# Up projections of two feed-forward layers in pairs of blocks by Strassen's seven products, with the inner tiles kept in memory and the layers split into an up phase and a down phase

## The reference, cut to what matters

```python
m = rms_norm(h, mlp_norm[i])
h = h + jnp.square(jax.nn.relu(m @ w_mlp_up[i])) @ w_mlp_down[i]
```

## Time and profile before

| | |
|---|---|
| time, median of 3 runs | 2839.71 us (2838.74 to 2841.25) |
| the profiled execution | 2841.24 us |
| its span, first to last instruction | 2839.6 us |
| PE busy | 2654.4 us, 93% of the span, 11982 matmuls |
| DVE busy | 1238.9 us, 44% |
| ACT busy | 795.4 us, 28% |
| DMA | 163.25 MB, mean 57 GB/s |
| granted TensorE clock, mean | 0.965 of 2.4 GHz |

### The profile page before, as it was taken

How to read it: one execution, slowest core, us unless ns; L and a number is a source line. 1 busy time by engine, 2 the same in 40 slices (tenths; PEclk the granted TensorE clock), 3 DMA queues, 4 the chain that set the end, 5 groups by cost and what they waited for, 6 DMA issues and landing times.

```text
span 2839.6 us, 31323 instructions
## 1 busy us (share of the span) xinstructions
PE 2654.4 (93%) x11982; PEld 2122.8 (75%) x11982; DVE 1238.9 (44%) x1443; ACT 795.4 (28%) x1115; POOL 61.8 (2%) x87
## 2 busy tenths in 40 slices
PE   7997598999999999999999878999999999999997
PEld 6776555568888888888878656888777788888885
DVE  5227627654423324234464554222576233242346
ACT  4212146652211101112243264111454011111123
POOL 1000000000000000000001200000000000000000
PEclk9998679999999999999999989999999999999998
DMA  5110000012111111111123100111333111111133
GB/s 198 37 37 19 1 0 1 1 60 81 45 52 45 52 52 44 52 44 52 52 82 138 50 0 23 52 45 51 134 104 119 52 45 52 44 52 51 45 126 111
DMA packets 45236, 163.25 MB, mean 57 GB/s; under 512 B 5088, under 2 KB 5120, under 8 KB 45136
## 3 DMA queue, kind: packets, MB, share of 16 engines
q1 hardware_dynamic: 35136, 125.84, 13.2%
q0 software_dynamic: 10032, 36.49, 3.6%
HBM read 144.89 MB, written 16.78 MB: 57 GB/s over the span
## 4 chain that ended last, share of the span: by engine, by line
PE 83%; DVE 8%; ACT 5%; issue 4%; DMA 0%; ACTq 0%; DVEq 0%; POOL 0%; POOLq 0%
PE ps L1681 68%; PE ps L2056 7%; PE ps L1833 1%; PE ps L1904 1%; ACT P L757 1%; PE ps L2010 1%; PE ps L1816 1%; PE ps L1830 1%; PE ps L1934 1%; PE ps L1914 1%; DVE w_lo L941 0%; PE ps L1840 0%; DVE Pb L1275 0%; DVE small L1460 0%; DVE S L1457 0%
## 5 line engine op out<-in xcount | busy, mean ns | idle before, releaser
L1681 PE MATMUL ps<-opP_hi,w_hi 128*128 128x512 f32 x1696 | 526.5, 392 | 5.4 <-DVE w_lo L941 3.8
L1681 PE MATMUL ps<-opP_lo,w_hi 128*128 128x512 f32 x1696 | 524.1, 390 | 0.0
L1681 PE MATMUL ps<-opP_hi,w_lo 128*128 128x512 f32 x1696 | 523.9, 390 | 0.0
L406 ACT ACTIVATE w_hi<-w_stage 128x1024 fp32r<-128x1024 f32 x228 | 239.2, 1049 | 600.3 <-PE ps L1681 598.2
L1681 PEld LDWEIGHTS ps<-opP_hi,w_hi 128*128 128x128 f32 x1696 | 319.4, 189 | 75.6 <-issue 9.8
L1681 PEld LDWEIGHTS ps<-opP_lo,w_hi 128*128 128x128 f32 x1696 | 319.8, 189 | 66.9
L1681 PEld LDWEIGHTS ps<-opP_hi,w_lo 128*128 128x128 f32 x1696 | 319.4, 188 | 66.8
L1681 PE MATMUL ps<-opQ_hi,w_hi 128*128 128x512 f32 x1152 | 357.1, 391 | 7.4 <-DVE w_lo L941 4.3
L1681 PE MATMUL ps<-opQ_hi,w_lo 128*128 128x512 f32 x1152 | 356.1, 390 | 0.0
L1681 PE MATMUL ps<-opQ_lo,w_hi 128*128 128x512 f32 x1152 | 355.8, 390 | 0.0
L941 DVE TENSOR_TENSOR w_lo<-w_stage,w_hi 128x1024 fp32r<-128x1024 f32 x228 | 278.3, 1221 | 100.5 <-ACT w_hi L406 100.2
(11 more groups left out here) (331 smaller groups left out, 2636.7 us busy)
## 6 DMA issues: line engine op xcount, KB each, us to landing
w_stage<-in_w_stream SPq DMA_DIRECT2D x228, 512.0 KB, 3.5
Xre<-x_spill POOLq DMA_DIRECT2D x16, 512.0 KB, 7.3
X<-in_xT POOLq DMA_DIRECT2D x8, 512.0 KB, 10.3
pp_spill<-ppout POOLq DMA_DIRECT2D x1, 4096.0 KB, 13.5
X<-in_xT SPq DMA_DIRECT2D x8, 512.0 KB, 4.4
T<-pp_spill POOLq DMA_DIRECT2D x8, 512.0 KB, 3.5
x_spill<-X POOLq DMA_DIRECT2D x1, 4096.0 KB, 15.1
x_spill<-X POOLq DMA_DIRECT2D x2, 2048.0 KB, 8.5
```

Source lines behind the costliest of these rows:

```text
L406: act.activation(w_hi[:, slot, :], w_stage[:, slot, :], ACT.Copy).then_inc(w_hi_done, 1)
L1681: mm = pe.matmul(ps[:, psum + half, :], weight, operand[:, k, half * HALF:(half + 1) * HALF], start=(begin and x == 0 and weight is wh and ...
```

## The change

Of each layer's up blocks, only the first 4 (layer 1) or the first 8, in halves (layer 2) stay as they are. The other 28 and 24 are taken in pairs. Two output tiles by two halves of the input features make a 2x2 block of the weights, and the two halves of the features by the two halves of the tokens make a 2x2 block of the activations; Strassen's scheme (the form with few additions) makes the 2x2 result from 7 products instead of 8. One product is 4 k-tiles by 3 forms, 12 matmuls of 128x512 in one bank.

- DVE forms 3 sums of the activations plus one in place for each layer (`form_sums`), once; and 4 sums of the weights for each pair (`weight_sum`). ACT and DVE split them into high and remainder (`weight_high`, `weight_low`, each 128x512, 7 for each pair, in place of two full blocks' `w_hi` and `w_lo`).
- DVE adds the products (`combine`, 7 of 128x512 for each pair, one operand in PSUM), ACT first copies one of them (`part_1`). DVE rectifies and scales in one instruction (`rectify`, 128x1024), ACT squares (`pair_square`).
- The squared tile goes from `T` to memory (`h_spill`), started by POOL (`spill`), 512 KB each, 32 tiles a layer. All up blocks and pairs of a layer come first, then all 32 down blocks in 4 chunks of 8; the 8 tiles of a chunk are read back by POOL's queue (`tiles_back`), those of chunk c+1 during chunk c, those of chunk 0 during the last pair, and are split by ACT (`tile_high`) and DVE (`tile_low`).
- The weights of a pair are kept in `X`, so the residual of layer 1 is written to `x_spill` during the w_out blocks, tile by tile, and read back during the last pair and after.
- In UPA ACT's rectify and copy and DVE's remainder go, and DVE's scaling becomes scale and rectify in one; in UPB likewise, and DVE and ACT get the sums and the first weights' parts to make, between the blocks.
- Operands P and Q change their places in the later stages, with the same instructions.

```diff
-B_PP, B_WIN, B_WOUT, B_MLP1 = 0, 2, 18, 26
-B_GATE, B_WIN2, B_MRG, B_WO2 = 90, 98, 108, 132
...
+FF_PLAIN, FF_PAIRS = (4, 8), (14, 12)
...
+            def spill(f, slot, cols=slice(0, S)):
+
+                counts[slot] += 1
+                if counts[slot] > 1:
+                    pool.wait_ge(spilled[slot], 16 * (counts[slot] - 1))
+                pool.dma_start(h_spill[f * P:(f + 1) * P, cols], T[:, slot, cols]).then_inc(spilled[slot], 16)
...
+                    if c == 0:
+                        if order == 0:
+                            pool.wait_ge(ff["lo"], pair_low_no(x, FF_PAIRS[x] - 1, 6))
+                        elif k in (0, 2, 4):
+                            pool.wait_ge(ff["mm"], product_no(x, FF_PAIRS[x] - 1, (1, 2, 4)[k // 2]))
...
+                    if c:
+                        pool.wait_ge(operand_ready, first + 8 * c + order - 1)
...
+            def pair_square(x, p, slot):
+                act.wait_ge(ff["relu"], 2 * pairs_before(x, p) + slot + 1)
+                act.activation(T[:, slot, :], T[:, slot, :], ACT.Square).then_inc(ff["square"], 1)
...
+            def pairs_act(x):
+                for p in range(FF_PAIRS[x]):
+                    weight_high(x, p, 6)
+                    if p:
+                        pair_square(x, p - 1, 1)
+                        act.wait_ge(ff["out"], out_no(x, p - 1, 3))
+                    act.wait_ge(ff["mm"], product_no(x, p, 0))
+                    act.activation(part_1[:, :], ps[:, pair_bank(x, p, 0), :], ACT.Copy).then_inc(ff["first"], 1)
+                    if p + 1 < FF_PAIRS[x]:
+                        for j in range(6):
+                            weight_high(x, p + 1, j)
+                    else:
+                        for order in range(DT):
+                            tile_high(x, HOME[order])
+                    pair_square(x, p, 0)
...
-                act.wait_ge(h0["lin"], n + 1)
-                act.activation(tt, tt, ACT.Relu).then_inc(h0["pos"], 1)
-                act.wait_ge(h0["pos"], n + 1)
-                act.activation(tt, tt, ACT.Square).then_inc(h0["relu"], 1)
-                ffa_high(0, n, n % 2)
...
+                if n == 2:
+                    for k in range(4):
+                        scaled_input(1, k)
+                if 2 <= n < 6:
+                    form_high(1, n - 2)
...
+                v.tensor_tensor(t1_raw[:, k, :], b, a, ALU.subtract).then_inc(ff["sum"], 1)
+                v.scalar_tensor_tensor(t3_raw[:, k, :], d, g, b, ALU.mult, ALU.subtract).then_inc(ff["sum"], 1)
+                v.wait_ge(ff["sum"], sum_no(x, k, 0))
+                v.scalar_tensor_tensor(t2_raw[:, k, :], d, g, t1_raw[:, k, :], ALU.mult, ALU.subtract).then_inc(ff["sum"], 1)
+                v.wait_ge(ff["sum"], sum_no(x, k, 2))
...
+            def slot_free(x, p, slot):
+                v.wait_ge(spilled[slot], 16 * (spills_before(x) + (FF_PLAIN[0] // 2, FF_PLAIN[1])[x] + p))
...
+            def pairs_dve(x):
+                for p in range(FF_PAIRS[x]):
+                    more = p + 1 < FF_PAIRS[x]
+                    if p:
+                        pair_end(x, p - 1)
+                    weight_low(x, p, 6)
+                    if more:
+                        weight_sum(x, p + 1, 0)
+                        weight_sum(x, p + 1, 1)
+                        weight_low(x, p + 1, 0)
+                    else:
+                        tile_low(x, 0, 0, HOME[0])
+                        tile_low(x, 0, 1, HOME[1])
+                    v.wait_ge(ff["first"], pairs_before(x, p) + 1)
+                    combine(x, p, sum_16[:, :], part_1[:, :], part(x, p, 1), 0, 1)
+                    if more:
+                        weight_low(x, p + 1, 1)
+                    combine(x, p, sum_165[:, :], sum_16[:, :], part(x, p, 2), 1, 2)
+                    if more:
+                        weight_low(x, p + 1, 2)
+                        weight_sum(x, p + 1, 2)
+                        weight_sum(x, p + 1, 3)
+                    else:
+                        tile_low(x, 0, 2, HOME[2])
+                    slot_free(x, p, 0)
...
+                    slot_free(x, p, 1)
+                    combine(x, p, T[:, 1, HALF:S], sum_16[:, :], part(x, p, 2), 4)
+                    if more:
+                        weight_low(x, p + 1, 4)
+                    combine(x, p, T[:, 0, HALF:S], sum_165[:, :], part(x, p, 5), 2, 5)
...
+                    rectify(x, p, 0)
+                    if more:
+                        weight_low(x, p + 1, 5)
+                    else:
+                        tile_low(x, 0, 4, HOME[4])
+                        tile_low(x, 0, 5, HOME[5])
...
+                if 2 <= n < 6:
+                    form_sums(1, n - 2)
+                    form_lows(1, n - 2)
+                if n == 6:
+                    first_pair(1, range(3))
+                if n == 7:
+                    first_pair(1, range(3, 6))
...
+            def pairs_pe(x):
+
+                for p in range(FF_PAIRS[x]):
+                    for j, (hi, lo, k0, c0) in enumerate(pair_forms):
+                        if p == 0 and j == 4:
+                            pe.wait_ge(evac_done, (B_DN1, B_DN2)[x])
+                            pe.wait_ge(ff["lo"], third_low_no(x, 3))
+                        if j == 0 and p >= 2:
+                            pe.wait_ge(ff["out"], out_no(x, p - 2, 7))
+                        elif j == 1 and p:
+                            pe.wait_ge(ff["first"], pairs_before(x, p))
+                        elif j and p:
+                            pe.wait_ge(ff["out"], out_no(x, p - 1, (1, 5, 3, 4, 6)[j - 2]))
+                        pe.wait_ge(ff["lo"], pair_low_no(x, p, j))
+                        for k in range(4):
+                            for weight, operand in ((form_hi[j], hi), (form_hi[j], lo), (form_lo[j], hi)):
+                                mm = pe.matmul(ps[:, pair_bank(x, p, j), :], weight[:, wcols(k)], operand[:, k0 + k, c0:c0 + HALF],
+                                               start=(k == 0 and weight is form_hi[j] and operand is hi),
+                                               stop=(k == 3 and weight is form_lo[j]))
+                        mm.then_inc(ff["mm"], 1)
+
...
+                    for n in range(DT):
+                        if n < 2:
+                            pe.wait_ge(ff["out"], out_no(x, FF_PAIRS[x] - 1, (5, 5)[n]))
+                        step(first + n, None, n, n % 2)
```

More of the change, by code:

```diff
@@ new lines, in _ @@
+            for f in range(FF_PLAIN[0]):
+                pool.wait_ge(ff["square"], f + 1)
+                spill(f, f % 2)
+            for p in range(FF_PAIRS[0] - 1):
+                pair_out(0, p, 0)
+                pair_out(0, p, 1)
+            for slot in range(2):
+                pool.wait_ge(spilled[slot], 16 * 4)
+            tiles_back(0, 0)
+            pool.wait_ge(s["spill"], 16 * DT)
+            pool.wait_ge(operand_hi, O_H1 + 6)
+            for k in range(4):
+                pool.dma_start(X[:, k, :], t["x_spill"][k * P:(k + 1) * P, :]).then_inc(tile_landed[k], 16)
@@ new lines, in down_act @@
+            def down_act(x, c):
+                first = (B_DN1, B_DN2)[x] + 8 * c
+                with act.Fori(0, 4) as i:
+                    for j in range(2):
+                        next_high(i * 2 + (first + j), i + first // 2, j)
+                        if c < 3:
+                            act.wait_ge(back[j], i * 16 + 16 * tile_turn(x, c + 1, 0))
+                            settle()
+                            act.activation(tile(h_hi[(c + 1) % 2], i * 2 + j), tile(h_raw[(c + 1) % 2], i * 2 + j), ACT.Copy)\
+                               .then_inc(operand_hi, 1)
@@ L697, in _, with down1 @@
+            third_form_high(0)
+            last_form_high(0)
+            pairs_act(0)
+            for c in range(3):
+                down_act(0, c)
+            def down1(b, turn, n, slot):
+                next_high(b, turn, slot)
+                act.wait_ge(evac_done, b + 1)
+                square_free(2, n)
+                high(opP_hi, tile(X, n), C_PLE, n)
+                square(tile(X, n), 2, n, True)
+            stream(act, B_DN1 + 24, 8, down1)
             next_high(B_GATE, B_GATE // 2, 0)
@@ new lines, in tile_low, with part, combine @@
+            def tile_low(x, c, order, k):
+                v.wait_ge(operand_hi, (O_H1, O_H2)[x] + 8 * c + order + 1)
+                v.tensor_tensor(h_lo[c % 2][:, k, :], h_raw[c % 2][:, k, :], h_hi[c % 2][:, k, :].bitcast(F32), ALU.subtract)\
+                 .then_inc(operand_ready, 1)
+            def part(x, p, j):
+                return ps[:, pair_bank(x, p, j), :]
+            def combine(x, p, out, a, b, after, product=None):
+                if product is not None:
+                    v.wait_ge(ff["mm"], product_no(x, p, product))
+                if after:
+                    v.wait_ge(ff["out"], out_no(x, p, after))
+                v.tensor_tensor(out, a, b, ALU.add).then_inc(ff["out"], 1)
```

(12 more changed lines are left out.)

685 lines of the change are left out of this document (434 added, 251 removed).

## The result

The changed kernel takes 2766.03 us (median of 4 runs, 2764.46 to 2767.58) where the kernel before takes 2839.73 beside it: ratio 0.9737, 95% interval 0.9725 to 0.975, so 73.7 us less. Its profiled execution took 2764.46 us, with a span of 2762.4.

A forecast was written before the change was run, and what follows sets the result against it. PE was taken as the bound in the feed-forward parts; -70.8 - 0.3 - 6.4 + 3.8 + 4 - 0.5 = -70.2 us took the profiled 2841.2 to 2771.0, or about 2770 as median, range 2758 to 2799.

The forecast's parts named there:

- 312 matmuls: Up blocks of both layers: 2496 matmuls become 2184, and those saved go at 0.2268 us each, -70.8 us.
- Layer 1's part: Start of layer 1's feed-forward part: one rectify step fewer ahead of the third up block's `w_lo`, -0.3 us.
- Pairs bound by PE: Pairs of both layers: PE needs 19.05 us a pair, DVE 14.9, ACT 7.1; hand-overs have slack and cost 0.
- UPA, -6.4: UPA to UPB's first block: six blocks take 32.7 us instead of 37.9 and the stage starts 1.2 earlier.
- the ring: UPA's period, scale through ACT and DVE steps back to scale: 6.25 us falls to 5.03, under PE's 5.44.
- UPB, +3.8: UPB: rounds of 7.7 us make PE wait before blocks 4 to 7; last ends at 2209.4 against 2205.6.
- Pair to down, +2 each: Last pair to first down block, twice: DVE reaches tile 4's remainder at 26.4 us, PE needs it at 24.8.
- Last stretch, -0.5: Last down chunk: its tile 7 no longer has a rectify in front, -0.5 us.
- Hand-overs cost: Rival: last pairs' DVE queue held up by landings, UPB and layer 1's start at upper bounds, +20 us; chance 0.18.
- A loss in every product: Rival: PE waits 0.15 to 0.3 us at each of 182 products, 27 to 55 us in all; chance 0.09.
- No change: Rival: a mixture in which losses just meet the gain, with no single mechanism; chance 0.02.
- The rival on the other side: Slower than before: spill landings hold up the pairs, gain gone at 12.5 us, 2907 us at 15; chance 0.05.

The follow-up runs named there:

- e1_eighth_product: Changed kernel with product 7 of each pair computed twice into the same bank, so 312 matmuls are back: 2831.16 us, ratio to before 0.9963.
- e2_upa_two_more: Changed kernel with two more ACT rectify instructions ahead of the square in each of the eight UPA blocks: 2771.69 us, ratio 0.976.
- e8_before_upa_once: Kernel before, with DVE scaling and rectifying in one instruction in UPA and ACT's rectify gone: 2833.81 us, ratio 0.9979.
- e9_before_dn0_by_tile: Kernel before, with layer 2's first down block waiting for its inner tiles one by one, not for all at its start: 2834.08 us, ratio 0.9981.
- e7_dve_8_more: Changed kernel with eight more DVE instructions (128x512, two inputs) in each pair but the last: 2802.7 us, ratio 0.9867.

## Why the prediction was right, and where its terms were off

2770 us was forecast, from 2758 to 2799, and 2766.0 came. On the profiled executions the sum said -70.2 and the traces say -76.8, of which 0.4 us are unchanged code. Term by term:

- *312 matmuls, -70.8.* Right. 0.2267 us in the pairs as in the blocks, and putting the twelve matmuls a pair back costs them again, less the waits that a longer pair hides (e1_eighth_product). Layer 1's part, -36.3, meets the sum's -38.1 - 0.3 + 2 to the tenth, and that is partly luck: the gap at the first down block costs 1.4 and not 2, and one that I had called hidden costs 0.5. There, at the third down block, `w_lo` stands in DVE's queue behind the remainder of the first tile of the next chunk, which DVE waits for 7.4 us. The Trainium skill gives 215.7 ns a matmul (TensorE: Matmul & The Clock Gate, "Wait — 56ns, not 53.3ns?"), by which the term would be an estimated 67.3; no stretch shown here runs at that distance.
- *Pairs bound by PE.* Right. DVE was put at 14.9 us of 19.05, 78%; it has 76 to 78%. The margin is now known: four more instructions are free, eight are not, and about 4.9 us of DVE time is what a pair has left.
- *UPA, -6.4; measured -7.9.* Mechanism right: the ring was the bound (e2_upa_two_more gives it back, e8_before_upa_once gives it alone). The block behind the standstill starts 1.35 us sooner (forecast 1.2), the six behind it take 5.1 us less (forecast 5.2). The failed step is "it takes 8.64 us, since the clock is down after the standstill, and still will": it takes 7.2 us, 1.5 less. Why is open. The standstill before it became shorter, 3.0 us against 4.43, but that is not the cause by itself: in e2_upa_two_more it is 4.37 and the block still takes 7.1.
- *UPB, +3.8; measured +2.8.* Mechanism right, gaps in front of blocks 4 to 7 as forecast, and none behind. The round is 7.39 us (2143.19 to 2150.58) and not 7.7, so a gap costs 1.95 us and not 2.2 (in brackets 1.6), since parts of the round are a tenth or two shorter than I took them. The upper bound, a falling clock in gaps of 2.2 us, did not come: 1.00 throughout.
- *Pair to down, +2 each; measured +1.4 each (1.1 in brackets).* The place was right, tile 4 of the first down block. The mis-sized step is the time at which DVE reaches that tile's remainder: 24.6 us after the last pair's start (at 1023.02 us in the trace) and not 26.4. The first tile is there when it was forecast, 9 us after the start. From then on DVE works through its queue with hardly a wait, 0.35 us in 14.4, so the work in front of tile 4 sets the time; the prediction's own prices for it, 6 remainders, 7 combines and 2 rectifies, make 14.6. What made it 26.4 the prediction doesn't show. The distance of queued landings, 1.8 us a tile from the earlier trace rows, was too large as well. ACT's copies of two of the tiles in the changed kernel, each just after its landing:

```profile
1009.15 1.06 ACT L902 ACTIVATE hA<-hA_raw 128x1024 fp32r<-128x1024 f32 x1 [0.51 <-DMA hA_raw<-h_spill]
1010.48 1.06 ACT L902 ACTIVATE hA<-hA_raw 128x1024 fp32r<-128x1024 f32 x1 [0.27 <-DMA hA_raw<-h_spill]
```

 They come 1.3 us apart, the next ones 1.3 to 1.6. Other traffic doesn't explain the difference: the stretch of the earlier trace rows has 320 GB/s and this one 318.
- *Last stretch, -0.5 beside the matmuls; measured 3 us more than -31.2.* This is the largest miss. About 1.9 of it is the low clock behind the 3.1 us wait, which e9_before_dn0_by_tile measures by taking the wait away; 0.6 is the smaller gap above, and 0.3 that the removed wait of 0.5 us cost 0.8. I had counted the wait at its length in UPB's term and nothing for what it leaves behind.

So nearly all the misses point the same way: the two largest are the clock behind a standstill, 1.5 us for a slow block taken as fixed and 1.9 for one counted at nothing, and the others are rounds and queues taken a little too slow. One slip of the prediction bears on nothing else: its bounds add up to 2759 to 2792 and not to 2795.

*The rivals.* Hand-overs cost 2 x 1.4, 0.5 and 2.8 us, about 6 and not 20. A loss in every product is refuted: no idle time of PE in 1128 matmuls, and none with four more DVE instructions. No change is out. The rival on the other side, the spill holding `slot_free` from a landing of 12.5 us on, did not come: in the pairs a spill lands in 3.5 and 2.9 us (medians of the two layers), at most in 8.7. The Trainium skill (SBUF — State Buffer, "SBUF: two separate sides") warns of transfers started by GpSimd beside a DVE in a two-port mode. DVE is busy for 76% here, with instructions that read two tensors, and none of the spills on POOL's queue comes near 12.5 us. The Trainium skill's fit for one such transfer (DMA: Bandwidth & Descriptors, "Anatomy of one DMA — SWDGE (gpsimd) path") gives an estimated 3.2 us for 512 KB. The spill's median over the whole execution, 3.1, agrees, and the reads' 3.7 is a little above. A longer landing was not tried, so the threshold of 12.5 us is argued and not shown. What e7_dve_8_more does show is the form such a loss would take: pairs whose helper is 0.83 us too slow cost 37 us in all.

*Left open.* What decides between 8.6 and 7.1 us for the slow block, and the -2.2 and +1.8 us in code that is the same, which are within what runs differ by.

## What to carry to other kernels

Where the chain of waits is one solid piece of PE work, a scheme that saves products is worth their number times the distance read in that piece, provided that each in-order helper queue has less work per unit than PE; check that by the unit's sum and by the work done ahead, because an overrun shows first when that work is used up, and most where the run of units ends. On a helper queue, put what the next block's weights need ahead of what only this block's result needs. Read the cost of a gap from the distance of the starts and not from the brackets. When you add or remove a standstill of PE, count the slow stretch behind it too: 1.9 us here behind 3.1.

## What the runs showed that I had not expected

- A removed wait pays more than its length: 3.1 us of waiting and 1.9 us, nearly all from a granted clock of 0.57 behind it. Gaps of 0.5 to 1.7 us, five in 34 us, left the clock at 1.00 and cost 0.3 us each beside their length.
- The length of a standstill does not say how long the slow block behind it is: 8.64 us for 24 matmuls behind 4.43 us, 7.32 behind 3.76, 7.2 behind 3.0, but 7.1 behind 4.37.
- PE goes on at full pace through the first pairs while its helper is 4% too slow, then at the helper's pace; 12.9 us more come due at the hand-over.
- Queued reads of 512 KB landed 1.3 to 1.6 us apart, against the 1.8 that I had worked out from another stretch with as much traffic.
